# Sparse attention with keys and values of each head's own, scores and bias made during the choice of keys, and 1/sum folded into the turning

## What is computed

```python
def dsa_mixer(h, rel_bias, w_in, g_cq, g_ckv, w_uq, w_uk, w_uv, w_qi, w_o):
    c_q, c_kv, k_idx, w_idx = jnp.split(h @ w_in, ...)
    c_q = rmsnorm(c_q, g_cq)
    c_kv = rmsnorm(c_kv, g_ckv)
    q = (c_q @ w_uq).reshape(B, T, A_HEADS, A_HEAD_DIM)
    q_lat = jnp.einsum('bthd,hdc->bthc', q, w_uk) * (A_HEAD_DIM ** -0.5)
    q_idx = (c_q @ w_qi).reshape(B, T, IDX_HEADS, IDX_DIM)
    # for each block of 128 queries:
        rel = jax.nn.relu(jnp.einsum('bqhd,bsd->bqhs', qb_idx, k_idx))
        score = jnp.einsum('bqh,bqhs->bqs', wb, rel)      # causal, else -inf
        _, sel = lax.top_k(score, n_sel)
        logits = einsum(qb_lat, kv_sel) + rel_bias[t5_bucket(dist)]
        p = jax.nn.softmax(logits, axis=-1)
        o_lat = jnp.einsum('bqhk,bqkc->bqhc', p, kv_sel)
    o = jnp.einsum('bthc,hcv->bthv', o_lat, w_uv)
    return o.reshape(B, T, -1) @ w_o
```

## Time and profile before

| | us |
|---|---|
| median of 3 runs (2881.3 to 2886.13) | 2886.11 |
| profiled execution, its span from first to last instruction | 2880.6 |
| index queries and index scores, PE from 2265.46 | to 2283.1 |
| choice of keys, DVE | 2289.9 to 2338.1 |
| loop of 40 steps, from the first sum on DVE to the first product with `w_o` | 2339.40 to 2434.34 |
| share of the span: PE, DVE, ACT, POOL busy | 95%, 66%, 41%, 19% |

### The profile page before, as it was taken

One profiled execution on the slowest core, in us unless ns is written; L12 is line 12 of the kernel. 1 busy time (PEld: TensorE's weight loads), 2 busy tenths in 40 slices (PEclk: granted clock), 3 DMA queues, 4 the chain that ended last, 5 costly groups with the idle time before them and its releaser, 6 DMA issues.

```text
span 2880.6 us, 36987 instructions
## 1 busy us (share of the span) xinstructions
PE 2750.5 (95%) x14045; PEld 2336.8 (81%) x14045; DVE 1890.1 (66%) x3534; ACT 1193.7 (41%) x1927; POOL 537.0 (19%) x393
## 2 busy tenths in 40 slices
PE   8999999989998999999998999999999989999997
PEld 6777878878876899998997888888888557788876
DVE  3334665765555778786985888888886585544434
ACT  5545243233223454547993333333333444322222
POOL 0122220220000778772000111111110011000000
PEclk9999999999999999999999999999999999999999
DMA  4112101003662677765668989898983201222220
GB/s 162 52 52 84 63 30 44 30 30 125 221 224 86 216 287 280 279 245 202 259 258 305 342 315 366 308 354 332 340 324 106 73 30 45 82 101 88 88 103 30
DMA packets 141359, 501.19 MB, mean 174 GB/s; under 512 B 13400, under 2 KB 67072, under 8 KB 111616
## 3 DMA queue, kind: packets, MB, share of 16 engines
q1 hardware_dynamic: 122752, 364.60, 35.5%
q0 software_dynamic: 18432, 134.23, 11.9%
HBM read 450.53 MB, written 48.25 MB: 173 GB/s over the span
## 4 chain that ended last, share of the span: by engine, by line
PE 79%; DVE 11%; ACT 4%; DMA 3%; issue 2%; POOL 1%; SPq 0%; DVEq 0%; ACTq 0%; POOLq 0%
PE bank L245 21%; PE bank L247 21%; PE bank L246 21%; DVE xn L1532 2%; PE bank L2154 2%; DMA w_raw<-in_w_in_dram 1%; PE bank L1107 1%; PE bank L1117 1%; PE bank L740 1%; PE bank L1123 1%; DVE M L2944 1%; DVE m L2940 1%; PE bank L347 1%; DVE whl L241 1%; PE bank L2742 1%
## 5 line engine op out<-in xcount | busy, mean ns | idle before, releaser
L245 PE MATMUL bank<-HH,uhl 128*128 128x384 f32 x1024 | 348.0, 340 | 1.9 <-POOL uhl L1658 1.9
L247 PE MATMUL bank<-HH,uhl 128*128 128x384 f32 x1024 | 345.0, 337 | 0.0
L246 PE MATMUL bank<-HL,uhl 128*128 128x384 f32 x1024 | 345.0, 337 | 0.0
L245 PE MATMUL bank<-vhl,awhl 128*128 128x512 f32 x768 | 300.1, 391 | 10.2 <-DVE awhl L2371 9.2
L247 PE MATMUL bank<-vhl,awhl 128*128 128x512 f32 x768 | 299.9, 390 | 0.0
L246 PE MATMUL bank<-vhl,awhl 128*128 128x512 f32 x768 | 299.7, 390 | 0.0
L1714 POOL DMA_INDIRECT gs<-in_uv_dram,idx x128 | 153.7, 1200 | 767.0 <-DVE x L1739 476.2
L2311 ACT ACTIVATE vhl<-vraw 128x1024 fp32r<-128x1024 f32 x128 | 135.8, 1061 | 314.8 <-PE bank L247 276.9
L1658 POOL TENSOR_TENSOR uhl<-ur,uhl 128x1024 fp32r<-128x1024 f32 x69 | 167.9, 2443 | 320.3 <-ACT uhl L1652 320.0
L245 PE MATMUL bank<-HH,whl 128*128 128x512 f32 x528 | 216.9, 411 | 3.0 <-DVE whl L241 3.0
L241 DVE TENSOR_TENSOR whl<-w_raw,whl 128x2048 fp32r<-128x2048 f32 x49 | 114.1, 2329 | 160.5 <-ACT whl L235 160.5
(11 more groups left out here) (421 smaller groups left out, 6249.1 us busy)
## 6 DMA issues: line engine op xcount, KB each, us to landing
ur<-in_peer_u_dram SPq DMA_DIRECT2D x128, 512.0 KB, 5.2
vraw<-in_peer_v_dram SPq DMA_DIRECT2D x128, 512.0 KB, 6.2
w_raw<-in_w_in_dram SPq DMA_DIRECT2D x36, 1024.0 KB, 5.0
xn<-in_ada_rows_dram SPq DMA_DIRECT2D x48, 512.0 KB, 4.6
g_scratch<-stg SPq DMA_DIRECT2D x12, 2048.0 KB, 8.4
gti<-g_scratch SPq DMA_DIRECT2D x16, 1536.0 KB, 12.0
wf_raw<-in_f_w_in_dram SPq DMA_DIRECT2D x22, 1024.0 KB, 4.8
act_scratch<-ag SPq DMA_DIRECT2D x96, 192.0 KB, 2.8
```

Of the source, the lines that this page charges most:

```text
L245: e.matmul(out, l[0], r[0], start=start, stop=False)
L246: e.matmul(out, l[0], r[1], start=False, stop=False)
L247: return e.matmul(out, l[1], r[0], start=False, stop=stop)
```

## The change

It does six things:

1. **Keys and values per head.** Instead of `QL` = q times `w_uk`, PE makes k of each head from the latent (`pe_up2`, what "k"), so a score needs one product of 128 rows instead of two. Instead of `ol` and `ov`, PE makes the values of all heads once (`pe_v`, 8 banks into `vkv`) and multiplies the turned tile by them (`pe_o`, four products of 512, 384, 256 and 128 columns). `crow` and `QL` go.
2. **All scores and the near bias before the loop.** Nine slots of 1280 columns hold the tiles; item g lies in slot h + 1 (`tile`), its turned form goes to slot h (`turned`). All 32 `pe_sc` and `act_sc` stand ahead of the loop, and POOL adds the bias into the tile (`pool_near`) as each arrives. The far bias, one number for a head, is subtracted from all buckets in `buckets()`, so that it need not be added. Four of the eight banks of values also stand ahead of the loop, and ACT's table load behind them.
3. **One DVE pass per item.** Query and bias are negated, and `dve_logits` adds `-M` and takes the minimum in one instruction (with a read of the accumulator) where there were two or three. `order` shows it as ISA.
4. **1/sum in the turning.** `dve_inv` takes two sums at a time; POOL makes a diagonal tile with the inverses (`pool_share`), and PE turns and scales by a true product with it (`pe_pt`), of which each head has ten, where there were transposes with the identity. It goes by key block `s_`, for all four blocks of the head, into one bank each of 512, 384, 256 and 128 columns; the first two are copied by DVE (`dve_pt`), the others by ACT.
5. **Index scores by head.** PE, ACT and DVE go through heads outside and blocks inside, and two of the four `qi` come later.
6. **Small.** `M0` is made by POOL at the start; `far_b` is not loaded; the `w_o` splits stand at steps 8, 9, 22 and 23; `w_uk` and `w_uv` are laid out anew on the host, as the other weights are.

```diff
-    def pe_ql(e, h):
-        for ct in range(2):
-            e.matmul(b[:, :], W3.tile(W_UK)[:, h * 256 + ct * P:h * 256 + (ct + 1) * P], rl[h % 3][:, :], start=True,
+    def pe_up2(e, h, what, W, x):
+        for k in range(2):
+            i = e.matmul(b[:, :], W3.tile(W)[:, k * D + h * P:k * D + (h + 1) * P], x[:, k, :], start=k == 0, stop=k == 1)
...
-        for ct in range(2):
-            i = e.matmul(b[:, 0:N], QL[:, h % 4, ct, blk(tb)], ckT[:, ct, 0:N], start=ct == 0, stop=ct == 1)
+        e.wait_ge(*A.of("k", h))
+        e.matmul(b[:, 0:N], qk2[:, h % 2, 0, blk(tb)], qk2[:, h % 2, 1, 0:N], start=True, stop=True).then_inc(*T.up("sc", g))
...
+    def dve_logits(e, g):
+        e.wait_ge(*G.of("near", g))
+        e.tensor_tensor_reduce(out=tile(g), in0=tile(g), in1=M[:, moff[tb]:moff[tb] + mw[tb]], scale=1.0, scalar=3.0e38,
+                               op0=ALU.add, op1=ALU.min, accum_out=st[:, 0, g:g + 1]).then_inc(*V.up("low", g))
...
+    def dve_inv(e, i):
+        e.wait_ge(*A.of("ex", 2 * i + 1))
+        e.reciprocal(st[:, 2, 2 * i:2 * i + 2], st[:, 1, 2 * i:2 * i + 2]).then_inc(*V.up("inv", i))
...
+    def pool_share(e, g):
+        e.wait_ge(*V.of("inv", g // 2))
+        e.tensor_scalar(dg[:, g % 8, :], ident, st[:, 2, g:g + 1], None, ALU.mult).then_inc(*G.up("share", g))
...
+    def pe_pt(e, h, s_):
+        if s_ == 0:
+            e.wait_ge(*G.of("share", 4 * h + 3))
+        for tb in range(s_, NT):
+            g = of_block(h, tb)
+            i = e.matmul(b[:, blk(tb - s_)], tile(g)[:, blk(s_)], dg[:, g % 8, :], start=True, stop=True)
...
+    def pe_o(e, h):
+        e.wait_ge(*V.of("pt", h, 1))
+        e.wait_ge(*A.of("pt", h, 3))
+        for s_ in range(NT):
+            i = e.matmul(b[:, s_ * P:S], vkv[:, s_, blk(h)], turned(h, s_), start=s_ == 0, stop=s_ == NT - 1,
...
         for s in range(STEPS):
+            if 4 <= s < 36:
+                pe_pt(e, s // 4 - 1, s % 4)
+            if s in (6, 10, 14, 18):
+                pe_v(e, (s - 6) // 4, 1)
+            if s % 4 == 1 and s >= 9:
+                pe_o(e, (s - 9) // 4)
...
         for s in range(STEPS):
             if s < NI:
+                dve_logits(e, s)
+            if s % 2 and 3 <= s < NI + 2:
+                dve_inv(e, (s - 3) // 2)
+            if 5 <= s < 37 and (s - 1) % 4 < 2:
+                dve_pt(e, (s - 1) // 4 - 1, (s - 1) % 4)
+            if s % 4 == 2 and s >= 10:
+                dve_o(e, (s - 10) // 4)
+            if s == 9:
+                split_lo(e, W3, W_O)
```

More of the change, by code:

```diff
@@ L2650, in act_ql @@
-    def act_ql(e, h):
-        T, A, V, G = DX
-        for ct in range(2):
[L2653 to L2657, removed]
+        if h >= 2:
+            e.wait_ge(*T.of("sc", 4 * (h - 2) + 3))
+        e.wait_ge(*T.of(what, h))
+        e.activation(qk2[:, h % 2, i, :], R9.bank(what, h)[:, :], ACT.Copy, scale=scale).then_inc(*R9.out(A, what, h))
@@ new lines, in pe_v, with act_v2 @@
+    def pe_v(e, s_, half):
+        T, A, V, G = DX
+        b = R9.take("v", s_, half)
+        for s in R9.empty("v", s_, half):
+            e.wait_ge(*s)
+        for k in range(2):
+            i = e.matmul(b[:, :], ckT[:, k, blk(s_)], W3.tile(W_UV)[:, k * D + half * 512:k * D + half * 512 + 512],
+                         start=k == 0, stop=k == 1)
+        i.then_inc(*T.up("v", s_, half))
+    def act_v2(e, s_, half):
+        T, A, V, G = DX
+        e.wait_ge(*T.of("v", s_, half))
+        e.activation(vkv[:, s_, half * 512:half * 512 + 512], R9.bank("v", s_, half)[:, :],
+                     ACT.Copy).then_inc(*R9.out(A, "v", s_, half))
@@ L2753, in pe_ov @@
-    def pe_ov(e, h):
-        T, A, V, G = DX
-        b = R9.take("ov", h)
-        for s in R9.empty("ov", h):
-            e.wait_ge(*s)
-        e.wait_ge(*W3.landed(W_UV))
-        e.wait_ge(*A.of("ol", h, 1))
-        for ct in range(2):
-            i = e.matmul(b[:, :], W3.tile(W_UV)[:, blk(2 * h + ct)], ol[h % 2][:, ct, :], start=ct == 0, stop=ct == 1)
-        i.then_inc(*T.up("ov", h))
-    def act_ov(e, h):
-        T, A, V, G = DX
-        e.wait_ge(*T.of("ov", h))
-        e.activation(HH[:, h, :], R9.bank("ov", h)[:, :], ACT.Copy).then_inc(*A.up("ov", h))
@@ new lines, in pe_pt, with act_pt @@
+    def pe_pt(e, h, s_):
+        T, A, V, G = DX
+        b = R9.take("pt", h, s_)
+        for s in R9.empty("pt", h, s_):
+            e.wait_ge(*s)
+        if s_ == 0:
[3 more added lines that the diff above has]
+            i = e.matmul(b[:, blk(tb - s_)], tile(g)[:, blk(s_)], dg[:, g % 8, :], start=True, stop=True)
+        i.then_inc(*T.up("pt", h, s_))
+    def act_pt(e, h, s_):
+        T, A, V, G = DX
+        e.wait_ge(*T.of("pt", h, s_))
+        e.activation(turned(h, s_), R9.bank("pt", h, s_)[:, 0:pw[s_]], ACT.Copy).then_inc(*R9.out(A, "pt", h, s_))
@@ L2873, in act_dsa @@
                 n += 1
-        for t2 in range(2):
-            e.wait_ge(*T.of("crow", t2))
-            e.activation(crow[:, 2 * t2:2 * t2 + 2, :], in2(R9.bank("crow", t2)), ACT.Copy).then_inc(*R9.out(A, "crow", t2))
-        for h in range(5):
-            if h < 4:
-                act_uq(e, h)
-            if h:
-                act_ql(e, h - 1)
+            if h in (1, 3):
+                act_qi((h + 3) // 2)
+        for h in range(2):
+            act_up2(e, h, "q", 0, -(P ** -0.5))
+            act_up2(e, h, "k", 1, 1.0)
         for g in range(4):
```

315 lines of the change are left out of this document (126 added, 189 removed).

## The result

The changed kernel is faster, by a little under half of what I forecast: a median of 2878.5 us against 2885.3 (13 runs of each), ratio 0.9977 with a 95% interval of 0.9969 to 0.9985, so 6.8 us where I forecast 15.1. The span of the profiled execution went from 2880.6 to 2872.4.

A forecast was written before the change was run, and what follows sets the result against it. The loop was taken as PE-bound, its lead-up as DVE-bound. After the change, first exponential at 2342.5 plus round-trip loop 66.9 plus surcharges 3 and 7 gives 2419.4, 15 us earlier: 2871 us, range 2852 to 2884.

The forecast's parts named there:

- the clean sum: Loop from first exponential to first w_o product, without surcharges: 4.6 + 54.4 + 7.9 = 66.9 us.
- a plain head: Loop: one head's round trip through five engines, from DVE's copy of 512 to the next, forecast at 7.85 us.
- PE up to the loop: Before the loop: PE's products from index queries through the first half of the values, summing to 75.0 us.
- my half of a covered product: Index scores on PE: 0.5 us saved at each of five head changes, giving 12.9 instead of 15.4 us.
- DVE's choice: Before the loop: key choice stays 48.3 us despite POOL's adds, ends at 2335.2, with 7 us to spare.
- The step that failed is POOL's: Loop: POOL's last two diagonal tiles on each head's path, 0.37 us each, 0.75 for both.
- The prediction's own test: Loop: forecast wrong if diagonal tiles took over 0.6 us, PE's queue let the next turning pass, or the clock stayed down.
- The surcharge for POOL and DVE: Loop: POOL's first two diagonal tiles and DVE's sums hinder each other, 0.4 us a head, 3 us in all.
- The surcharge for the clock: Loop: PE's clock at half speed for four stretches of 3.4 us after pauses, 7 us, between 0 and 14.
- rival 4: Loop: change works, but the round trip is 1 to 2 us a head longer, 2879 to 2886 us; chance 0.11.
- The two rules: Trainium skill: two-input VectorE instructions conflict with GpSimd reading SBUF, single-input ones don't; pauses in a loop lower PE's clock.
- rival 2: Loop: PE's clock stays at 1.2 GHz throughout, 30 us for eight heads in place of 7, 2894 us; chance 0.08.

The follow-up runs named there:

- e4: Changed kernel with DVE making the diagonal tiles and extra PE products filling PE's waits; loop 67.7 us, median 2859.7 us, ratio 0.9909.
- e6: Changed kernel with index heads in the order 0, 2, 4, 6, 1, 3, 5, 7; loop 89.1 us, median 2884.6 us, ratio 0.9997.
- e2: Changed kernel with extra f32 products of 512 columns keeping PE at work ahead of each head's turning; loop 76.0 us, median 2864.4 us, ratio 0.9928.
- e1: Changed kernel with the diagonal tiles made by DVE instead of POOL; loop 76.8 us, median 2865.1 us, ratio 0.9930.
- e12: Changed kernel with only the high and low part of a head's output placed three steps later; loop 68.5 us, median 2859.6 us, ratio 0.9916.
- e8: e4 with the output's high and low part three steps later and fewer extra products; loop 58.5 us, median 2849.0 us, ratio 0.9868.
- e11: e8 with earlier table load and exponentials, first tile pair by POOL's select, no extra PE products; loop 60.7 us, median 2846.4 us, ratio 0.9865.
- e5: Changed kernel with POOL making the diagonal tiles by a select instead of a scaled copy; loop 75.8 us, median 2865.2 us, ratio 0.9925.
- e7: Changed kernel without diagonal tiles: DVE scales the score tiles and PE turns them with the identity; loop 76.8 us, median 2868.1 us, ratio 0.9938.

## Why the prediction was right and wrong

- **The place and the mechanism** were right: the end moved with the first `w_o` product, and the loop is one round trip through DVE, ACT, POOL and PE. With POOL and the clock taken out (e4) it takes 67.7, where the clean sum said 66.9. Both numbers are a little softer than they look: the terms of a plain head as written add up to 7.72 and not to 7.85, about 0.8 us over the loop, and in e4 two differences cancel, as said there.
- **PE up to the loop**: 75.0 forecast, 72.7 measured (2266.41 to the end of the values at 2339.1). The term that was off is the index scores, 10.0 in place of 12.9; my half of a covered product at a change of head was too little, e6 has 0.8 to 1.1 us. First exponential 74.7 from the start, forecast 77.0: 2.4 gained.
- **DVE's choice**: 48.2 us (2287.80 to 2336.0), as forecast, beside POOL's 20 us of adds. It had 5 us to spare, not 7.
- **The step that failed is POOL's**: "since it has one input I take 0.37, so 0.75 for both". A tile takes 0.58 with nothing beside it (2.34 for four in the last head), and 1.10 for the first of four where DVE's two-input sums run beside it, 2.85 in all. As the first two need 1.7 us and the two 1/sums of a head are 0.9 apart, the last pair queues behind the first, which I had left out of the path: 2.4 us from the second 1/sum to the turning in place of 1.07. With the clock at 1.00 (e2) a plain head takes 8.96 and not 7.85, and the loop 76.0 and not 66.9: 9.1 lost, of which 8.3 go when DVE makes the tiles (e4). The upper bound of 0.48, from an addition with two inputs, was none: that row was only the nearest. The prediction's own test ("wrong if the diagonal tiles took over 0.6 us") held: they took 0.71 on average.
- **The surcharge for POOL and DVE**, 3: DVE's sums were hardly slowed (0.70 for 512 columns with POOL at work, 0.69 in e4 without; 0.77 once, behind the split of head 5). The other side pays: POOL's first tile, 0.5 a head, inside the 9.1.
- **The surcharge for the clock**, 7: it cost 10.4 (e2), within its 0 to 14. I had four stretches of 3.4, there were six, two of them twice as long, and little of this is the first error's doing: with DVE's faster tiles (e1) the clock was still low for 24 us of 27.

The sum: 2.4 gained before the loop, 9.1 lost to the tiles, 3.4 to the clock, 3 not lost on DVE: 7.1 less than forecast, 7.8 in place of 14.9. In the median the miss is 7.5 us (2878.5 for 2871); it lies 6.1 above the span here, where I had added 5.5. The result lies in rival 4's range of times (2879 to 2886) within a microsecond, and "slower diagonals" stands in its list; its 0.11 was too low for an operation of which the trace had no row.

The two rules. In head 5 DVE's split of 2.29 started at 2390.57; POOL's first tile, begun before it, took 0.60, and its second, begun at 2390.76, took 2.69 (timelines of POOL and DVE):

```profile
2390.18 3.27 POOL L2711 TENSOR_SCALAR dg<-cst,st 128x128 f32<-128x128 f32 x2 [7.83 <-DVE st L2704]
...
2390.57 2.29 DVE L241 TENSOR_TENSOR wfhl<-wf_raw,wfhl 128x2048 fp32r<-128x2048 f32 x1 [0.56 <-ACT wfhl L235]
```

Two tiles take 3.27 there, 1.18 elsewhere. The Trainium skill's rule (SBUF — State Buffer, "Who interferes with whom") has the one that comes second wait, whichever it is; the trace agrees for POOL's second tile, and I had applied the rule in one direction only. I had also told it without the proviso that this section of the Trainium skill makes for VectorE's two-port modes, and it matters here: the scaling of 512 columns has a single input, and it took longer beside POOL's additions all the same (last section). On the clock, the Trainium skill's loop whose pauses bring the clock down again and again (TensorE: Matmul & The Clock Gate, "HAM oscillation — how this bites in real kernels") is what the changed kernel shows, six times in eight heads, though never for the whole loop as in my rival 2.

## What to carry to other kernels

Where a step is moved to an engine and an operation that the trace has no row for, and it stands in a round trip that repeats, its price times the number of trips is the largest unknown: take it with a wide bound, and count everything queued ahead of it on that engine. In a loop that is one round trip, look at where each engine's in-order list waits for another while it still has work for the trip: moving two calls by three steps took 17.9 us off the loop (e12), 9.2 at full clock (e8 against e4), where the whole change had brought 7.8. Pauses that PE didn't have before also cost what its clock loses behind them, and they go with the pauses (e11).

## What the hardware showed that I had not expected

- The same 128x128 f32 tile costs POOL 0.58 us as a scaled copy of a tile, 0.27 as a select along the diagonal of a spread column (e5, both with nothing beside them), and DVE 0.20 (e1).
- DVE's f32 scaling of 512 columns takes 0.48 with POOL idle (e7); with POOL's additions beside it the same operation took 0.885 in the kernel before (its groups in the loop):

```profile
L2713 DVE TENSOR_SCALAR lm<-lm,st 128x512 f32<-128x512 f32 x8 | 7.1, 885 | 0.3
```

- Where DVE's two-input pass started first, POOL's tile beside it took longer and DVE's pass did not: 1.10 in place of 0.60 beside a sum of 0.70, 2.69 beside the split of 2.29. In the kernel before, where POOL was already at work, it was DVE's sum that took longer.
- Pauses of PE of 2.7 us were followed by a low clock in one place (from 2383.1) and not in another (2373.48), and in e12 a pause of 2.2 was followed by one (2364.8 to 2368.4). Which of them are is not settled here; all pauses under 2 us in e11 left the clock at 1.00.
